# Value product of a windowed attention in two column halves, and the second mixer's lower weight parts on VectorE with u times c formed straight from its bank

## The reference

```
# first mixer: windowed attention, query blocks of 128, each sees 2 or 3 key blocks of 128
probs = jax.nn.softmax(jnp.concatenate([scores, sink_col], axis=-1), axis=-1)[..., :-1]
out = jnp.einsum('bnhrqk,bnkhd->bnqhrd', probs.astype(v.dtype), vb)

# second mixer: z = rms_norm_2(x) @ w_in, cut into seven pieces of 512 columns
y_hgrn = (o_h.reshape(b_, s_, HGRN_W) * jax.nn.silu(zg)).astype(x.dtype)
y_conv = zb * causal_depthwise_conv(zc * zu, conv_w[l])       # 3 taps, 512 channels
x = x + jnp.concatenate([y_hgrn, y_conv], axis=-1) @ w_out[l]
```

## Time and profile before

| What | us |
| --- | --- |
| three runs | 2527.86, 2532.95, 2536.98 |
| median | 2532.95 |
| profiled execution: its time | 2534.28 |
| profiled execution: span, first to last instruction | 2532.5 |
| PE busy in it | 2462.1 |
| DVE, ACT, POOL busy in it | 1247.7, 1005.0, 394.6 |

### The profile page before, as it was taken

How to read it: one execution, slowest core, us unless ns; L and a number is a source line. 1 busy time by engine, 2 the same in 40 slices (tenths; PEclk the granted TensorE clock), 3 DMA queues, 4 the chain that set the end, 5 groups by cost and what they waited for, 6 DMA issues and landing times.

```text
span 2532.5 us, 29084 instructions
## 1 busy us (share of the span) xinstructions
PE 2462.1 (97%) x11416; PEld 1986.0 (78%) x11416; DVE 1247.7 (49%) x1843; ACT 1005.0 (40%) x1632; POOL 394.6 (16%) x283
## 2 busy tenths in 40 slices
PE   8999999898999999999999999999999999999998
PEld 7766668676888887888888788888887787888886
DVE  5577744457776454533333433423576644444422
ACT  6666653335455233423223322322634333332321
POOL 0000000054410010111102211101455300111101
PEclk9999999999999999999999999999999999999999
DMA  5221225223446331333332233322321222333231
GB/s 183 86 59 49 77 93 188 85 95 106 150 134 216 108 133 50 97 94 93 100 107 93 78 98 100 100 92 92 99 67 51 89 103 67 100 100 98 93 101 50
DMA packets 171337, 251.56 MB, mean 99 GB/s; under 512 B 11201, under 2 KB 88257, under 8 KB 171201
## 3 DMA queue, kind: packets, MB, share of 16 engines
q1 hardware_dynamic: 170768, 248.92, 31.0%
q10 hardware_dynamic: 432, 0.79, 0.1%
HBM read 231.83 MB, written 16.78 MB: 98 GB/s over the span
## 4 chain that ended last, share of the span: by engine, by line
PE 81%; DVE 8%; issue 5%; ACT 4%; DMA 1%; POOL 1%; POOLq 0%; SPq 0%; ACTq 0%; DVEq 0%
PE bank L1058 80%; DVE W L1817 1%; DVE T L1825 1%; DVE wlo L1817 1%; DMA scr_z<-T 1%; ACT whi L1384 1%; PE bank L1161 0%; ACT pr L1479 0%; DVE SC L2428 0%; DVE pr L1928 0%; POOL acc L2511 0%; ACT qs L1384 0%; DMA zb<-scr_z 0%; DVE T L1817 0%; ACT xp L1684 0%
## 5 line engine op out<-in xcount | busy, mean ns | idle before, releaser
L1058 PE MATMUL bank<-xh,whi 128*128 128x512 f32 x1784 | 716.2, 401 | 11.1 <-DVE wlo L1817 10.6
L1058 PE MATMUL bank<-xh,wlo 128*128 128x512 f32 x1784 | 698.5, 392 | 0.0
L1058 PE MATMUL bank<-xl,whi 128*128 128x512 f32 x1784 | 698.0, 391 | 0.0
L1817 DVE TENSOR_TENSOR wlo<-raw,whi 128x1024 fp32r<-128x1024 f32 (+2 forms) x382 | 472.4, 1241 | 332.3 <-ACT whi L1384 332.1
L1384 ACT ACTIVATE whi<-raw 128x1024 fp32r<-128x1024 f32 (+2 forms) x406 | 419.9, 1039 | 539.4 <-PE bank L1058 530.4
L1058 PEld LDWEIGHTS bank<-xh,whi 128*128 128x128 f32 x1784 | 337.1, 189 | 105.5 <-issue 27.2
L1058 PEld LDWEIGHTS bank<-xh,wlo 128*128 128x128 f32 x1784 | 336.7, 189 | 72.2
L1058 PEld LDWEIGHTS bank<-xl,whi 128*128 128x128 f32 x1784 | 337.5, 189 | 66.1 <-issue 1.0
L1817 DVE TENSOR_TENSOR T<-bank,R 128x512 f32<-128x512 f32 x90 | 61.8, 688 | 341.7 <-PE bank L1058 341.7
L1058 PE MATMUL bank<-hh,whi 128*128 128x512 f32 x528 | 205.4, 389 | 0.0
L1058 PE MATMUL bank<-hl,whi 128*128 128x512 f32 x528 | 205.4, 389 | 0.0
(11 more groups left out here) (340 smaller groups left out, 3614.2 us busy)
## 6 DMA issues: line engine op xcount, KB each, us to landing
raw<-in_w_in SPq DMA_DIRECT2D x92, 512.0 KB, 3.6
raw<-in_w_ffn_in SPq DMA_DIRECT2D x88, 256.0 KB, 3.2
raw<-in_ffn_gate SPq DMA_DIRECT2D x88, 256.0 KB, 2.8
raw<-in_ffn_up SPq DMA_DIRECT2D x88, 256.0 KB, 3.1
raw<-in_ffn_down SPq DMA_DIRECT2D x44, 512.0 KB, 3.5
raw<-in_w_ffn_out SPq DMA_DIRECT2D x22, 512.0 KB, 3.5
raw<-in_w_xattn_kv SPq DMA_DIRECT2D x16, 512.0 KB, 4.1
raw<-in_w_kv_mem SPq DMA_DIRECT2D x16, 512.0 KB, 4.0
```

The lines of the kernel that those rows point to most:

```text
L1058: return e.matmul(out, l, r, start=start, stop=stop, skip_group_check=skip)
L1817: return e.tensor_tensor(out, a, b, op)
```

## The change

1. `pv`: each product of a key block is cut in two matmuls of 256 moving columns. The first takes heads 0 and 2 of the four (each 128 columns of `pt`) and writes partitions 0 to 63 of the bank, the second takes heads 1 and 3 and writes partitions 64 to 127. Both load the same 64 columns of `v`, into array columns 0 to 63 and 64 to 127. `o_out` is then one ACT copy of 128 partitions x 256 instead of two of 64 x 256.
2. The 24 `w_lo` of the second mixer that POOL did are done by DVE; POOL's `weight` is gone. Their places in `ORDER` stay.
3. `c_out` multiplies with R2 = R times R, made once on DVE, and `u_out` is one instruction, T = bank times `cu`. The first tap of the convolution is a scaled copy on ACT (`u_first`), the other two are added on DVE one point later, straight in `cu`; POOL's copy is gone.

```diff
-        def weights(name, pieces, nk, X, lo="dve", nat=False, ntok=S, order=None):
+        def weights(name, pieces, nk, X, nat=False, ntok=S, order=None):
...
-            weights(n, columns("w_in_2", i), 8, "mix2", "dve" if n == "hf" else "pool", nat=n == "hi")
+            weights(n, columns("w_in_2", i), 8, "mix2", nat=n == "hi")
...
             def conv():
-                tmp.new("uc", m)
-                step("u_conv", m)
+                step("u_first", m)
+                soon(1, "u_conv", m)
...
-                    ins = mm(b[0:64, :], v[:, k0 + j, kv * 64:kv * 64 + 64], pt[j][:], j == 0, j == k1 - k0 - 1)
+                    x = pt[j][:].rearrange("p (a b q) -> p a b q", a=2, b=2)
+                    for half in range(2):
+                        ins = mm(b[64 * half:64 * half + 64, 0:256], v[:, k0 + j, kv * 64:kv * 64 + 64], x[:, :, half, :],
+                                 j == 0, j == k1 - k0 - 1)
...
-                src = b[0:64, :].rearrange("p (a b q) -> p a b q", a=2, b=2)
                 w.wait_ge(*at("pv", i))
-                copy(q[0:64, 2 * kv:2 * kv + 2, chunk(n)], src[:, :, 0, :]).then_inc(*up("o_out", ("o half", i)))
-                copy(q[64:128, 2 * kv:2 * kv + 2, chunk(n)], src[:, :, 1, :]).then_inc(
+                copy(q[:, 2 * kv:2 * kv + 2, chunk(n)], b[:, 0:256].rearrange("p (a q) -> p a q", a=2)).then_inc(
                     *up("o_out", ("o out", i), ("side", "free", u)))
...
+            def u_first(m):
+
+                n, t = tmp("u", m)
+                w.wait_ge(*at("u out", m))
+                copy(cu[:, m, :], t[:], V("cw2", 3 * m + 2)).then_inc(*up("u_first", ("u conv", m, 0)))
...
             def c_out(m):
                 u, b = main("hc", m)
-                w.wait_ge(*at("R", "mix2"))
+                if m == 0:
+                    w.wait_ge(*at("R", "mix2"))
+                    tt(R2[:], R[:], R[:], ALU.mult).then_inc(*up("mixer2_in", ("R2",)))
+                w.wait_ge(*at("R2"))
                 w.wait_ge(*at("full", "hc", m))
-                tt(cu[:, m, :], b[:], R[:], ALU.mult).then_inc(*up("mixer2_in", ("c out", m), ("main", "free", u)))
+                tt(cu[:, m, :], b[:], R2[:], ALU.mult).then_inc(*up("mixer2_in", ("c out", m), ("main", "free", u)))
...
-                tt(t[:], b[:], R[:], ALU.mult).then_inc(*up("mixer2_in", ("u out", m), ("main", "free", u)))
-                w.wait_ge(*at("u out", m))
-                w.wait_ge(*at("c out", m))
-                tt(cu[:, m, :], cu[:, m, :], t[:], ALU.mult).then_inc(*up("mixer2_in", ("u in", m), ("tmp", "free", n)))
+                tt(t[:], b[:], cu[:, m, :], ALU.mult).then_inc(*up("mixer2_in", ("u out", m), ("main", "free", u)))
...
-                ts(t[:], u, k2, None, ALU.mult).then_inc(*up("u_conv", ("u conv", m, 0)))
...
-                stt(t[:, 2:S], u[:, 0:S - 2], k0, t[:, 2:S], ALU.mult, ALU.add).then_inc(*up("u_conv", ("u conv", m, 2)))
+                stt(c[:, 2:S], t[:, 0:S - 2], k0, c[:, 2:S], ALU.mult, ALU.add).then_inc(
+                    *up("u_conv", ("u conv", m, 2), ("tmp", "free", n)))
```

More of the change, by code:

```diff
@@ L234, in build @@
         slots, G = [], {}
-        def weights(name, pieces, nk, X, lo="dve", nat=False, ntok=S, order=None):
+        def weights(name, pieces, nk, X, nat=False, ntok=S, order=None):
             n = sum(p[2] for p in pieces)
             ids = list(range(len(slots), len(slots) + nk // 2))
-            slots.extend((pieces, k, lo) for k in order or range(0, nk, 2))
+            slots.extend((pieces, k) for k in order or range(0, nk, 2))
             G[name] = dict(ids=ids, n=n, X=X, nat=nat, ntok=ntok, M=ntok // P if nat else n // P)
@@ L1801, in scalar @@
                     "ffn_up": ffn_up, "bounds": bounds, "f_sig": f_sig, "f_log": f_log, "h_silu": h_silu,
-                    "i_out": i_out, "b_split": b_split, "level": level, "ends": ends, "ke_turn": ke_turn,
+                    "i_out": i_out, "u_first": u_first, "b_split": b_split, "level": level, "ends": ends, "ke_turn": ke_turn,
                     "h_read": h_read, "h_rms": lambda h: rms("h", h), "h_gate": h_gate, "fin_gain": fin_gain}
@@ L2358, in u_out @@
                 w.wait_ge(*free(tmp, "tmp", n))
+                w.wait_ge(*at("c out", m))
                 w.wait_ge(*at("full", "hu", m))
[L2360 to L2363 removed]
+                tt(t[:], b[:], cu[:, m, :], ALU.mult).then_inc(*up("mixer2_in", ("u out", m), ("main", "free", u)))
             def u_conv(m):
[L2366 to L2371 removed]
+                n, t = tmp("u", m)
+                c = cu[:, m, :]
+                k0, k1 = (V("cw2", 3 * m + j) for j in range(2))
                 w.wait_ge(*at("u conv", m, 0))
[L2373 removed]
+                stt(c[:, 1:S], t[:, 0:S - 1], k1, c[:, 1:S], ALU.mult, ALU.add).then_inc(*up("u_conv", ("u conv", m, 1)))
                 w.wait_ge(*at("u conv", m, 1))
[L2375 removed]
+                stt(c[:, 2:S], t[:, 0:S - 2], k0, c[:, 2:S], ALU.mult, ALU.add).then_inc(
+                    *up("u_conv", ("u conv", m, 2), ("tmp", "free", n)))
             def b_out(m):
@@ L2511, in tt @@
                 return e.tensor_tensor(out, a, b, op)
-            def weight(i):
-                pieces, k, lo = slots[i]
-                if lo != "pool":
-                    return
-                n = sum(x[2] for x in pieces)
-                w.wait_ge(*at("w hi", i))
-                tt(wlo[i % NH][:, :, 0:n], raw[i % NR][:, :, 0:n], whi[i % NH][:, :, 0:n].bitcast(F32), ALU.subtract).then_inc(
-                    *up("w_lo_pool", ("w lo", i)))
             def square(tag, k):
@@ L2600, in ffn_gate @@
                 tt(t[:], t[:], R[:], ALU.mult).then_inc(*up("ffn_gate", ("ffn gate", tag, j)))
-            def u_conv(m):
-                n, t = tmp("uc", m)
-                w.wait_ge(*at("u conv", m, 2))
-                e.tensor_copy(cu[:, m, :], t[:]).then_inc(*up("conv2_pool", ("u there", m), ("tmp", "free", n)))
             def b_out(m):
                 n, t = tmp("b", m)
-                w.wait_ge(*at("u there", m))
+                w.wait_ge(*at("u conv", m, 2))
                 w.wait_ge(*at("b in", m))
@@ L2641, in out @@
                 tt(xT[:, k, :], xT[:, k, :], R[:], ALU.mult).then_inc(*up("out_pool", ("out", k)))
-            does = {"w_lo": weight, "square": square, "weigh": weigh, "state": state_,
-                    "skip_x": skip_x, "across": across_, "ffn_gate": ffn_gate, "u_conv": u_conv, "b_out": b_out,
+            does = {"square": square, "weigh": weigh, "state": state_,
+                    "skip_x": skip_x, "across": across_, "ffn_gate": ffn_gate, "b_out": b_out,
                     "level_mul": level_mul, "ends": ends, "h_gate": h_gate, "out": out}
```

15 lines of the change are left out of this document (4 added, 11 removed).

## The result

The changed kernel takes 2505.27 us, the median of four runs (2503.15 to 2507.25); before, in the same session, 2530.72 us (2527.86 to 2536.98). The ratio is 0.9896, 95% interval 0.9874 to 0.9918: faster by 1.0%, 25.4 us. The profiled execution took 2503.15 us, with a span of 2501.3 us, against 2534.28 before, so the two profiles are 31.1 us apart, 5.7 us more than the medians. One run of the kernel before, beside the first four experiments, took 3074.78 us at a granted clock of 0.75; the ratios leave it out.

A forecast was written before the change was run, and what follows sets the result against it. PE, busy for 2462 of 2532.5 us, was taken as the bound. 2534.3 - 15.0 (value products) - 8 (second mixer) = 2511.3 us, the median 1.3 us lower, so 2510; own range 2503 to 2516, full range 2503 to 2526.

The forecast's parts named there:

- Part 1, the streams: Attention's value products: column halves run side by side, shortening PE's stream over 16 blocks by 16.8 us.
- New waits in the attention: Softmax and conv on DVE and ACT get less time, so PE's 3.4 us idle there grows by 1.8 us.
- (a): Second mixer: PE's 4.2 us wait before 1958.34 us shrinks by 4.0 us as DVE's run before it shortens.
- (b): Second mixer: the last `choose` wait, 2.5 us before 1974.70, shrinks by 1.2 us; a blocked scaled copy goes, a lower part comes.
- (c): Second mixer: the five other `choose` waits, 3.5 us together, shrink by 2.0 us.
- (e): Second mixer: the wait for `vi` loses 0.5 us, as three lower parts join DVE's queue and wait for `whi`.
- The charge of +2 for DVE's further load: Second mixer: 2 us charged for 11 us more DVE work that must find room, and for unplaced `whi` waits.
- (f): Second mixer: of some 4 us lost at the lower clock behind long waits, 2.2 us come back.
- serial halves: Rival: the value products' halves run one after another, giving 0 to +5.6 us there; time 2526 us, chance 0.13.
- Exposed loads: Rival: the value products' halves pair but each record waits 0.14 us for its weight load; gain 6 us, 2519 us, chance 0.08.
- No relief in the mixer: Rival: second mixer's waits for DVE only change cause, its edits give 0 to 2 us; 2516 to 2518 us, chance 0.10.
- DVE's queue as the bound: Rival: in the second mixer's levels, lower parts queued on DVE delay each level 2.27 us; about 2554 us, chance 0.05.

The follow-up runs named there:

- the first four experiments: The first batch of follow-up runs; the kernel before, measured again beside them, took 2532.11 us (22 runs).
- part 1 alone: The kernel before with only the value products in column halves and the single copy to `q`: 2517.38 us, ratio 0.9947.
- part 2 alone: The full change without the column halves, so both second-mixer edits together (lower parts on DVE; u, c and taps): 2519.93 us, ratio 0.9956.
- stand-ins: The full change plus, on POOL at each of the 24 lower-part places, two 128x512 subtractions that nobody reads: 2527.68 us, ratio 0.9988.
- the run on the same columns: The full change with both halves on array columns 0 to 63, one after the other, and two copies to `q`: 2519.68 us, ratio 0.9958.
- one-input copies: The full change plus, on POOL at each of the 24 lower-part places, four 128x512 one-input copies that nobody reads: 2525.1 us, ratio 0.9972.

## Why the prediction was right

The prediction was 2510 us with its own range of 2503 to 2516; 2505.27 us lies in both ranges. 2.2 of the 4.7 us between them are the kernel before, whose runs now have a median of 2530.72 instead of 2532.95. The change gave 25.4 us where 23 were predicted: 14.7 against 15.0 for part 1 alone, 12.2 against 8 for part 2 alone. The mechanisms are those that were forecast, but that the sum came out within 2.4 us is partly luck: the new waits in the attention took back 2.3 us more than was allowed for them, and part 2 gave 4 us more. That part 1 alone came so close to 15.0 is luck too, since its profile shows 12.0.

- **Part 1, the streams, -16.8.** 17.0. The step on which all hung, that column halves pair like the row halves of the earlier trace rows, is shown: starts 7 ns apart, and a gain that is gone when the columns are the same. The copies to `q` became 16 of 380 ns, as said. The rule of the Trainium skill that was weighed there ("TensorE: Matmul & The Clock Gate", "Part 3: Packing small matmuls") would have given 6 us of gain; for this product the trace does not bear it out: pairs follow each other at 216 ns, so the weight loads stay hidden.
- **New waits in the attention, +1.8.** Too small: 4.1, to 7.4 us of idle time, above the 6 us that were named as a sign.
- **(a) the long wait, -4.0.** -4.2, gone, by the edit of u and c alone, as worked out there.
- **(b) the last masked copy, -1.2.** -2.5, gone too. The edit of u and c alone takes 2.0 of it.
- **(c) the five others, -2.0.** -1.4: 3.5 us became 2.1, with the one of the third head grown from 0.9 to 1.3.
- **(d) `hq`, -0.9.** -0.9, gone, by the lower parts alone.
- **(e) `vi`, +0.5.** Nothing: 1.9 us as before.
- **The charge of +2 for DVE's further load.** This is a mis-sized term. The load was put at +11 us, and DVE is busy for 1.7 us more. The step that failed is the share of the blocking: POOL's lower parts were given 58% of the excess, by their part of POOL's busy time, 14 us with the scaled copies. The subtractions alone lost 56 x (801 - 468) = 18.6 of their 21 us of excess: nearly all of it was the lower parts. With only those moved, DVE has 24 x 1.33 = 32 us more of them and is 5.2 us busier, so 27 us of blocking went, not 14. Little was left to charge for. With the lower parts alone on DVE the subtractions already fall to 468 ns.
- **(f) the clock, -2.2.** The other mis-sized term. PE's busy time for the same records fell by 5.6 us in the profile of the full change and by 5.7 in that of the mixer's parts alone, by 3.1 and 3.0 with either of them, and it is 9.0 higher with the stand-ins than without. It went with the waits, by some 0.6 us for each us of idle time, where 2.2 us were expected for about 9. Each is a single execution, and chance has a part in it: with part 1 alone, in the same code as before, it is 1.6 us less at 0.9 us more idle time.

In idle time (a) to (e), with 0.2 more for `W`, gave 8.9 us where 7.6 less the charge were expected, and the clock up to 5.6 where 2.2 were. By the runs it is less, 12.2 instead of 14.5 us together; which of the two falls short there, the runs cannot say. Nor do they part, in the change itself, VectorE's shorter instructions from POOL's level products coming earlier once its lower parts are gone.

The rivals: **serial halves** is what the run on the same columns is (2519.68 us), and the changed kernel is not that. **Exposed loads** fails by the spacing of 216 ns. **No relief in the mixer** fails by the 12.2 us of that part alone. **DVE's queue as the bound**: no wait for `wlo` appears on PE in the mixer, and lower parts alone make the kernel 5.4 us faster. Its outcome does exist, but not through its mechanism: it takes POOL's work kept beside DVE's lower parts to make the mixer 8.6 us longer than before.

## What to carry to other kernels

Where a product fills only half of the array's columns and its stream is what costs, cut it in two halves of columns that stand next to each other in the order; then look for the waits of the engines that had only just been in time. Before an operation is left with GpSimd because it has time, add up what VectorE's two-input instructions on SBUF take above their free length: here moving 58.7 us of work from GpSimd to VectorE, together with the edit of u and c, made VectorE 1.7 us busier and PE's waits 8.9 us shorter. And count the low-clock intervals of two profiles before a difference of 2 us in an untouched stretch is explained.

## What the runs showed of the hardware that was not expected

- Two float32 products on the same rows and disjoint columns start 7 ns apart and run at full rate. PE also pairs them when three records stand between them in the order, but not when five do (1.02 us for the block with two key blocks, 1.92 instead of 1.44 with three). So its matmuls did not all start in the order in which they were issued.
- GpSimd's one-input copies hold up VectorE's two-input subtractions nearly as much as its two-input instructions do (736 and 771 ns on average, 468 without either; a pair of them 1.58 instead of 0.8 us), and are held up by VectorE in turn. An instruction with its second input in a bank is not (masked copy 0.75 us). Idle work at 24 places cost 18 to 22 us of the kernel.
- More short waits of TensorE went with a longer busy time and mostly a lower clock (1.00 to 0.96): over six versions its busy time for the same 1060 records of the mixer was 195.8, 198.4, 198.4, 201.5, 202.1 and 204.9 us with idle times of 4.7, 8.1, 10.1, 13.5, 15.8 and 18.7 us (full change, u and c alone, lower parts alone, before, one-input copies, stand-ins), one execution each. The kernel with part 1 alone lies off this row, 199.9 us with 14.4.
- The granted clock falls to its lower level for a few us at a time, and in stretches that are the same in both kernels one execution has such an interval where another has none (0.95 against 0.98, 0.96 against 1.00). In such untouched stretches the two profiles here differ by 2.9 us.
